# Padding in front of the feed-forward buffers of a float32 transformer kernel

## The reference, cut to what matters

```python
def swiglu_ffn(h, w_gu, w_down):
    gate, up = jnp.split(h @ w_gu, 2, axis=-1)          # 1024 -> 2 x 2816
    return (jax.nn.silu(gate) * up) @ w_down            # 2816 -> 1024
...
        x = x + 0.5 * swiglu_ffn(rms_norm(x, norm_g[i, 0]), ffn_w_gu[i, 0], ffn_w_down[i, 0])
```

## The kernel before

| buffer | start | over a multiple of 2048 |
|---|---|---|
| `whi`, `wlo` (all) | 49280 to 77952 | 128 |
| `xT`, `xh`, `xl` | 82048, 98432, 114816 | 128 |
| `par` (596 bytes), `cst` (1536) | 131200, 131808 | 128, 736 |
| `rb`, `lnb`, `sqs`, `sq` | from 133344 | 224 |
| `small` (384), `ada` (96) | 141536, 141920 | 224, 608 |
| `ffn0_ah` and `ffn2_ah` | 142016 | 704 |
| `ffn1_ah`, `ffn3_ah` | 150208, 160448 | 704 |
| `al`, `g0`, `g1`, `u0`, `u1` of each block | behind `ah` | 704 |
| `hyb_rgh`, `hyb_igh`, `hyb_xcl`, `hyb_thl` | 142016 to 166592 | 704 |
| most of `dif_*`, for one `dif_qb`, `dif_sq` | from 165568 | 1728 |

## Time and profile before

### The profile page before, as it was taken

The page is one execution under the profiler, slowest core; times in us unless marked ns, Lnnn a source line. Parts: engine busy times, 40 slices in busy tenths (PEclk is TensorE's granted clock), DMA queues, the critical chain, the costliest instruction groups (busy, mean ns, idle before and its releaser), DMA issues.

```text
span 2265.5 us, 24782 instructions
## 1 busy us (share of the span) xinstructions
PE 2229.3 (98%) x9878; PEld 1789.8 (79%) x9878; DVE 1262.5 (56%) x1956; ACT 916.8 (40%) x1443; POOL 154.6 (7%) x128
## 2 busy tenths in 40 slices
PE   7999999999999999999999999999899999999999
PEld 6888888877688888888888887777678888877777
DVE  6443445878655434454433446777566535555863
ACT  4322233666533222333322335777533222237672
POOL 2000003000040000030000021000130000020000
PEclk9999999999999999999999999999999999999999
DMA  6323214131124233132223223222134434242221
GB/s 190 100 75 124 93 52 156 38 94 56 39 96 168 84 102 112 65 121 93 93 93 112 79 89 110 72 73 91 50 116 152 142 117 130 89 130 69 63 74 38
DMA packets 201763, 217.40 MB, mean 96 GB/s; under 512 B 4984, under 2 KB 194552, under 8 KB 201648
## 3 DMA queue, kind: packets, MB, share of 16 engines
q1 hardware_dynamic: 194960, 193.48, 26.3%
q0 software_dynamic: 6544, 22.26, 2.9%
q10 hardware_dynamic: 144, 0.08, 0.0%
HBM read 213.66 MB, written 6.32 MB: 97 GB/s over the span
## 4 chain that ended last, share of the span: by engine, by line
PE 93%; DVE 3%; ACT 3%; issue 1%; DMA 0%; SPq 0%; DVEq 0%; ACTq 0%
PE ps L1599 91%; PE ps L1603 1%; DVE sb_wlo L1085 0%; ACT sb_xh L636 0%; ACT sb_whi L636 0%; DMA sb_raw<-ffn_w_gu 0%; DVE sb_xl L1090 0%; ACT sb_hyb_th L636 0%; ACT sb_lnb L636 0%; DVE sb_xl L1389 0%; DVE sb_lnb L1579 0%; DVE sb_dif_p L1375 0%; DVE sb_hyb_rq L1488 0%; DVE sb_rb L1581 0%; DVE sb_hyb_q L1502 0%
## 5 line engine op out<-in xcount | busy, mean ns | idle before, releaser
L1599 PE MATMUL ps<-sb_xh,sb_whi 128*128 128x512 f32 x2120 | 846.1, 399 | 25.3 <-DVE sb_xl L1090 10.7
L1599 PE MATMUL ps<-sb_xh,sb_wlo 128*128 128x512 f32 x2120 | 829.3, 391 | 0.0
L1599 PE MATMUL ps<-sb_xl,sb_whi 128*128 128x512 f32 x2120 | 828.9, 391 | 0.0
L1085 DVE TENSOR_TENSOR sb_wlo<-sb_raw,sb_whi 128x1024 fp32r<-128x1024 f32 (+2 forms) x401 | 474.4, 1187 | 488.3 <-ACT sb_whi L636 487.1
L636 ACT ACTIVATE sb_whi<-sb_raw 128x1024 fp32r<-128x1024 f32 (+2 forms) x401 | 386.7, 968 | 576.9 <-PE ps L1599 570.3
L1599 PEld LDWEIGHTS ps<-sb_xh,sb_whi 128*128 128x128 f32 x2120 | 400.0, 189 | 118.8 <-issue 17.3
L1599 PEld LDWEIGHTS ps<-sb_xh,sb_wlo 128*128 128x128 f32 x2120 | 400.0, 189 | 85.8
L1599 PEld LDWEIGHTS ps<-sb_xl,sb_whi 128*128 128x128 f32 x2120 | 400.4, 189 | 84.6 <-issue 4.6
L1599 PE MATMUL ps<-sb_ffn_ah,sb_whi 128*128 128x512 f32 x704 | 277.6, 394 | 0.0
L1599 PE MATMUL ps<-sb_ffn_ah,sb_wlo 128*128 128x512 f32 x704 | 276.0, 392 | 0.0
L1599 PE MATMUL ps<-sb_ffn_al,sb_whi 128*128 128x512 f32 x704 | 273.3, 388 | 0.0
(11 more groups left out here) (254 smaller groups left out, 1764.6 us busy)
## 6 DMA issues: line engine op xcount, KB each, us to landing
sb_raw<-ffn_w_gu SPq DMA_DIRECT2D x86, 1024.0 KB, 5.2
sb_raw<-ffn_w_down SPq DMA_DIRECT2D x32, 1024.0 KB, 4.9
sb_raw<-gla_w_in SPq DMA_DIRECT2D x12, 1024.0 KB, 5.3
sb_raw<-diff_w_in SPq DMA_DIRECT2D x12, 1024.0 KB, 5.1
sb_ada_raw<-w_ada POOLq DMA_DIRECT2D x12, 1024.0 KB, 6.2
sb_raw<-w_in SPq DMA_DIRECT2D x10, 1024.0 KB, 5.2
sb_raw<-ffn_w_down SPq DMA_DIRECT2D x16, 512.0 KB, 3.7
sb_raw<-ffn_w_down SPq DMA_DIRECT2D x16, 256.0 KB, 2.7
```

Source lines behind the costliest of these rows:

```text
L1085: e.tensor_tensor(lo, raw[panel % NRAW][:, 0:nk, off:off + 128], hi.bitcast(F32), ALU.subtract).then_inc(sem["w_lo"], 1)
L1599: return e.matmul(out, lhsT, rhs, start=start, stop=stop, skip_group_check=skip)
```

## The change

Each feed-forward block's scope gets a buffer that nothing reads or writes, ahead of `ah`. Its size is computed from the number of columns of `par`, `cst`, `small` and `ada`: 149 + 384 + 96 + 24 = 653 words, so `PAD` is 371 words, 1484 bytes. No instruction is added, removed or moved.

```diff
+PAD = -(NCOLS + 3 * 128 + 96 + 24) % 512
...
         def ffn_memory(f, mem):
+
+            sb(f"ffn{f}_pad", [128, PAD], F32, mem)
             return (sb(f"ffn{f}_ah", [128, 12, S], F32R, mem), sb(f"ffn{f}_al", [128, 12, S], F32R, mem),
                     [sb(f"ffn{f}_g{i}", [128, S], F32, mem) for i in range(2)],
                     [sb(f"ffn{f}_u{i}", [128, S], F32, mem) for i in range(2)])
```

## The result

The change makes the kernel slower: 2275.16 us median of 5 runs (2274.58 to 2276.11) against 2266.76 us median of 5 (2265.84 to 2267.17). The ratio is 1.0041, 95% interval 1.003 to 1.0053: a small loss, but clear of the noise. The forecast was 2266.1 us in a range of 2261.0 to 2270.0, so the time lies outside it, on the side that had 0.13.

The account below looks back on a forecast made before the run. TensorE's matmul pitch was taken to bound the kernel. VectorE/ScalarE, TensorE and transitions, 0 + 0 + 0, left the profiled 2267.3 us unchanged; the median lies 1.2 us lower, so 2266.1 us, range 2261.0 to 2270.0.

Parts of the forecast that it names:

- What bounds the kernel: In feed-forward blocks, only TensorE's pitch between matmul starts can move the end; block 2's chain is 1591 matmuls without a wait.
- The map: In the memory map, the pad puts `ah` at 143520, so tiles go from 704 to 160 over a multiple of 2048.
- VectorE and ScalarE on the moved tiles: Six instructions per hidden tile in the feed-forward blocks: 0 expected, bounds minus 9 to plus 9 ns for each.
- TensorE on the moved tiles: 2112 down matmuls on the chain: pitch unchanged, 0 expected, between 4.6 us less and 4.4 us more.
- reading by boundaries of 128 bytes: For the down matmuls' moving tiles, starts at 160 and 704 are both misaligned to 128 bytes, so the pitch stays, 0.
- the upper bound: Down matmuls slow at most to 0.2311 each, as 9 matmuls behind a stall, from 0.2290: 4.4 us more.
- distance and region: High-to-low tile distance or lying above byte 142016 might explain the slower down pitch; the change alters neither, so 0.
- The transitions: Uneven matmuls between down and gate/up stretches: 0 expected, 0.4 us in all at most, either way.
- The slower rival: Down matmuls on TensorE cut one more 64-byte piece each: 4.6 us more, to 2270.7 us; chance 0.13.
- The full gain: Down pitch falls to 0.2268 by place against weights or true multiples of 2048: 4.6 us less, 2261.5 us; chance 0.18.

Follow-up runs that it names:

- The narrow kernel: Against the kernel before, down matmuls load 64 of 128 weight columns and write 64 of 128 output rows, with four differently padded blocks; 2270.52 us, one run.

## Why the prediction was wrong

**What bounds the kernel** held: in the blocks TensorE's pitch was the only thing to move, and it moved the end.

**The map** held to the byte: 160, by the base of 128 and two roundings.

**VectorE and ScalarE on the moved tiles**, taken at 0: right. Their means are within 1 ns of before.

**TensorE on the moved tiles**, taken at 0: this step failed. It measured 4.4 ns x 2112 = 9.3 us. Two things in it were wrong. The choice of 0 rested on a reading by boundaries of 128 bytes, where 160 and 704 are equally misaligned; the runs show a difference from the weights modulo 256, by which 704 is at 64 (2.2 ns) and 160 at 32 (6.6 ns). And the upper bound, 0.2311 from the uneven stream behind a stall, was too low: 0.2333 is a steady pitch that no stream of such tiles has in the trace of before. That the stream behind a stall should bound a change of address was never shown. I also weighed distance and region as reasons for no change, and neither has any effect (0.2290 at a distance of 32768, 0.2267 above byte 142016).

**The transitions**, taken at 0: right. The gate/up stretch that begins with one takes 108.84 us after the change and 108.85 before.

**The slower rival** had the right sign, place and engine, and half the price (4.6 us). Its mechanism, one more piece of 64 bytes, is refuted: a start at 0 cuts none and is as slow.

**The full gain** had one half right, that the place against the weights counts, which I wrote down and didn't follow to what 32 bytes off would cost. Its other half, that a true multiple of 2048 would bring the gain, is refuted by the kernel that does just that.

**What it means by cause.** Shown, by moving either side: the pitch of these fp32r matmuls depends on the moving tiles' start minus the weight tiles' start modulo 256, when the high and low tiles of a side have the same offset, to within 1 ns from block to block. Only argued: that reads of the moving tile and of a weight load collide. The narrow kernel changed the weights and the output rows together, so it doesn't show that the load is the other party. Open: which load meets which matmul, and why 64 is cheaper than most others.

## What to carry to other kernels

Where matmuls run back to back, compute the pitch per stretch from the timeline and compare stretches of the same shape: 2 ns in 227 showed an effect that no wait, busy share or duration points to. Before padding buffers, read the memory map, since the first buffer's base and the allocator's rounding enter the sum; and match moving and stationary tiles to each other, not to a round number. When a trace shows that place matters but not how, an offset that isn't in the trace has no bound from it, and the range must say so.

## What the runs showed of the hardware that I had not expected

Pitch of a stream of fp32r matmuls of 128 x 512 with a weight load of 128 columns for each, at the 2.4 GHz level, by the moving tile's start minus the weights' modulo 256 bytes:

| difference | pitch, us |
|---|---|
| 0 | 0.2267 |
| 4 | 0.2381 |
| 8 | 0.2326 |
| 16 | 0.2317 |
| 32, 128, 192, 224 | 0.2333 |
| 64 | 0.2289 |
| 96 (block 3) | 0.2336 |
| 160 (block 3) | 0.2345 |

In block 3 other matmuls stand between, which adds some 0.3 ns (0.2292 there against 0.2289 in the kernel before). That brings 96 to 0.2333, but leaves 160 about 0.9 ns above it. At 128, block 3 of the kernel with true multiples of 2048 had 0.2327, so the table holds to about 1 ns. The offsets below 32 and the 160 were measured in one kernel, run once.

The matmuls that move `xh` and `xl`, about three quarters of this kind, happened to be matched. Where they were not, in the kernel with moved weights, the whole took 2302.33 us in its one run, against 2266.54 before: 32 bytes between two buffers are worth 1.6% of this kernel.
